# Norm, modulation and router between the output projection and the experts, rebuilt by token, and the last norm joined to the expert rounds

## The reference, cut to what matters

```python
xl = xl + ml[2][:, None] * (merged @ w_out)
h = rms_norm(xl, norm_ffn) * (1 + ml[4]) + ml[3]            # shift and scale differ for context and latent tokens
scores = sigmoid(h @ w_router)                              # 16 experts in 4 groups
# best group by the sum of its top two biased scores, two experts in it, weights normalised
xl = xl + ml[5][:, None] * moe_ffn(h, ...)
y = rms_norm(xl, norm_final)
```

## Time and profile before

| | |
|---|---|
| median of 3 runs | 2398.67 us (2397.53 to 2400.23) |
| the profiled execution | 2402.82 us, of which span 2401.0 us |
| PE, PEld busy | 2188.6 us (91%), 1892.9 us (79%) |
| DVE, ACT, POOL busy | 1483.2, 1143.3, 8.2 us |
| mean granted clock of PE | 0.963 |
| HBM read, written | 453.88 MB, 3.98 MB |

### The profile page before, as it was taken

One profiled execution on the slowest core, in us unless ns is written; L12 is line 12 of the kernel. 1 busy time (PEld: TensorE's weight loads), 2 busy tenths in 40 slices (PEclk: granted clock), 3 DMA queues, 4 the chain that ended last, 5 costly groups with the idle time before them and its releaser, 6 DMA issues. The chain is left out here.

```text
span 2401.0 us, 28904 instructions
## 1 busy us (share of the span) xinstructions
PE 2188.6 (91%) x11236; PEld 1892.9 (79%) x11236; DVE 1483.2 (62%) x2021; ACT 1143.3 (48%) x1534; POOL 8.2 (0%) x12
## 2 busy tenths in 40 slices
PE   7799999999999999998899969965999999999993
PEld 4499988977777899997799968855877777777772
DVE  6967576346544444443544444555678879879984
ACT  6733565333444434332343333332567667667760
POOL 1000000000000000000000000000000000000000
PEclk9899999999999999998999989997899999999996
DMA  9844333433333455543355555520589889889981
GB/s 353 288 148 140 105 139 102 138 123 119 114 115 113 149 179 183 176 167 110 125 182 180 188 177 193 181 90 21 206 287 339 297 287 345 278 309 336 333 294 55
DMA packets 127287, 459.92 MB, mean 192 GB/s; under 512 B 15456, under 2 KB 17280, under 8 KB 126880
## 3 DMA queue, kind: packets, MB, share of 16 engines
q1 hardware_dynamic: 127136, 457.92, 55.3%
HBM read 453.88 MB, written 3.98 MB: 191 GB/s over the span
## 5 line engine op out<-in xcount | busy, mean ns | idle before, releaser
L161 DVE TENSOR_TENSOR wlo<-raw,whi 128x1024 fp32r<-128x1024 f32 x832 | 1006.5, 1223 | 734.7 <-ACT whi L155 720.0
L155 ACT ACTIVATE whi<-raw 128x1024 fp32r<-128x1024 f32 x832 | 870.6, 1058 | 918.6 <-PE bank L173 669.7
L171 PE MATMUL bank<-hhi,whi 128*128 128x384 f32 x1664 | 567.2, 341 | 29.1 <-DVEq L1519 16.9
L173 PE MATMUL bank<-hhi,wlo 128*128 128x384 f32 x1664 | 559.8, 336 | 0.0
L172 PE MATMUL bank<-hlo,whi 128*128 128x384 f32 x1664 | 559.4, 336 | 0.0
L171 PEld LDWEIGHTS bank<-hhi,whi 128*128 128x128 f32 x1664 | 315.2, 189 | 48.5 <-issue 24.9
L172 PEld LDWEIGHTS bank<-hlo,whi 128*128 128x128 f32 x1664 | 315.1, 189 | 1.8
L173 PEld LDWEIGHTS bank<-hhi,wlo 128*128 128x128 f32 x1664 | 314.6, 189 | 0.0
L1994 PE MATMUL bank<-whi,group_hi 128*128 128x512 f32 x512 | 203.6, 398 | 5.3 <-DVE wlo L161 4.0
L1996 PE MATMUL bank<-wlo,group_hi 128*128 128x512 f32 x512 | 201.5, 394 | 0.0
L1995 PE MATMUL bank<-whi,group_lo 128*128 128x512 f32 x512 | 200.5, 392 | 0.0
(11 more groups left out here) (320 smaller groups left out, 2414.6 us busy)
## 6 DMA issues: line engine op xcount, KB each, us to landing
raw<-in_dense SPq DMA_DIRECT2D x448, 512.0 KB, 3.7
raw<-in_moe SPq DMA_DIRECT2D x384, 512.0 KB, 5.0
merged<-in_x SPq DMA_DIRECT2D x8, 768.0 KB, 6.4
cs_rows_bc<-cs_rows SPq DMA_DIRECT2D x8, 768.0 KB, 5.0
out_y<-merged SPq DMA_DIRECT2D x4, 768.0 KB, 3.3
pool_w_sb<-in_pool_w SPq DMA_DIRECT2D x1, 1024.0 KB, 6.2
w_router_sb<-in_w_router SPq DMA_DIRECT2D x1, 1024.0 KB, 4.5
pool_inv_count<-in_pool_inv SPq DMA_DIRECT2D x1, 768.0 KB, 4.3
```

The source lines that it names most:

```text
L155: self.nc.scalar.activation(self.whi[:, n % W, :], self.raw[:, n % R, :], ACT.Copy).then_inc(self.hi_done, 1)
L161: self.nc.vector.tensor_tensor(self.wlo[:, n % W, :], self.raw[:, n % R, :], self.whi[:, n % W, :].bitcast(F32), ALU.subtract).then_inc(se ...
L171: self.nc.tensor.matmul(out, self.whi[:, s, c], xhi[:, k, :], start=(k == 0), stop=False)
L173: last = self.nc.tensor.matmul(out, self.wlo[:, s, c], xhi[:, k, :], start=False, stop=(k == blocks - 1))
```

## The change

1. `w_out_phase`, `norm_phase("ffn")`, `modulate_phase` and `router_phase` become one block, the new `out_phase`. As each block of x is finished within the passes, ACT squares it and writes `u = x * a` (two Copies with a scale for each partition), and DVE adds the squares into one 128x384 sum.
2. After the last tile PE needs three one-column products for the sum over features, now one number for each token in its partition, and rsqrt works on 128x3.
3. 24 units (two feature blocks by 128 tokens): PE multiplies u by `turn` = [identity | w_router], 144 columns, so a unit is token-major u beside its part of the logits; one STT of DVE multiplies by rstd and adds the shift, ACT writes `hhi` and the logit parts, DVE `hlo`. A reduction over 16 parts gives the logits; the chain of choices is as before, without `lows` between its steps.
4. The shift is needed with the features in the columns: it is turned by PE, stored to HBM (16 KB) and loaded back broadcast to all partitions (two DMAs of 1 MB, pieces of 512 B). w_router is loaded as 16 columns of its rows (pieces of 64 B). The shift's share of the logits is computed in pass 1.
5. A round is one block: `pick`, `place` and the slot weights are built in its head. Its tail squares each block of x when it is added (ACT), sums by a float32 product with ones (PE, between the scatters), then makes rsqrt, y and the stores. Rounds 1 and 2 come after that.

```diff
+def out_phase(N, E):
+        @block.sync
+            for s in range(iters * body):
+                N.load(sp, N.tile0 + s + R)
+                if s == 1:
+                    sp.dma_start(E.turn[:, :, P:P + NE], io.w_router[:, :, 0:NE]).then_inc(s_ld, 16)
...
+                if s == 4:
+                    sp.wait_ge(s_rows, 1)
+                    sp.dma_start(flat.rearrange("(q f) -> q f", f=P), E.rows[:, :]).then_inc(s_st, 16)
+                if s == 7:
+                    sp.wait_ge(s_st, 16)
+                    for g in range(2):
+                        sp.dma_start(E.shift[:, g, :, 0:P],
+                                     flat.rearrange("(k g f) -> g k f", g=2, f=P)[g].partition_broadcast(P)).then_inc(s_shift, 16)
...
+        @block.scalar
+            def of_block(m):
+                act.wait_ge(s_x, 4 + 2 * (m + 1))
+                if m >= 2:
+                    act.wait_ge(s_acc, max(1, m - 2))
+                A(E.xsq[:, m % 2, :], xt[:, m, :], ACT.Square).then_inc(s_sq, 1)
+                for g, (lo, hi) in enumerate(SEG):
+                    A(E.u[:, m, lo:hi], xt[:, m, lo:hi], ACT.Copy, scale=N.mod_a[:, m, g:g + 1]).then_inc(s_u, 1)
+            for i in range(iters):
+                for t in range(body):
+                    N.act_hi(act, i, body, t)
...
+                    if i == 0 and t == 3:
+                        A(E.turn[:, :, 0:P], N.ident[:, :].unsqueeze(1).to_broadcast([P, KB, P]), ACT.Copy).then_inc(s_turn, 1)
...
+                    if t - 1 in own_end:
+                        of_block(4 * i + own_end.index(t - 1))
...
+            for n, (q, c) in enumerate(units):
+                act.wait_ge(s_h, n + 1)
+                A(N.hhi[:, 2 * q:2 * q + 2, c * P:(c + 1) * P], E.h[:, n % 4, :, 0:P], ACT.Copy).then_inc(s_hh, 1)
+                A(E.lgp[:, c * NE:(c + 1) * NE, 2 * q:2 * q + 2].rearrange("p e a -> p a e"), E.h[:, n % 4, :, P:P + NE], ACT.Copy)\
+                    .then_inc(s_lg, 1)
...
+        @block.vector
+            for n, (q, c) in enumerate(units):
+                dve.wait_ge(s_mm, n + 1)
...
+                V.scalar_tensor_tensor(out=E.h[:, n % 4, :, :], in0=two(B[ring[q % 2][c]][:, 0:2 * (P + NE)]), scalar=E.ry[:, c:c + 1],
+                                       in1=E.shift[:, seg(c), 2 * q:2 * q + 2, :], op0=ALU.mult, op1=ALU.add).then_inc(s_h, 1)
+                if n >= 2:
+                    low(n - 2)
...
+            V.reduce_sum(E.lt[:, :], E.lgp[:, :, :], AX).then_inc(s_lt, 1)
+            dve.wait_ge(s_ex, 1)
...
+        @block.tensor
+                for b in range(2):
+                    last = mm(bank[:, b * (P + NE):(b + 1) * (P + NE)], E.u[:, 2 * q + b, c * P:(c + 1) * P], E.turn[:, 2 * q + b, :],
+                              start=True, stop=True)
+                last.then_inc(s_mm, 1)
+                if n == 2:
+                    pe.wait_ge(s_acc, KB - 1)
+                    pe.wait_ge(s_x, 2 * KB + 4)
+                    for cc in range(NCH):
+                        last = mm(B[1][:, cc:cc + 1], E.acc[:, cc * P:(cc + 1) * P], N.ones[:, 0:1], start=True, stop=True)
+                    last.then_inc(s_sum, 1)
...
 def expert_round(N, E, r):
+                for lo, hi in ((0, 4), (4, 8), (8, 12), (12, 14), (14, 16)):
+                    sp.wait_ge(E.s_y, KB * r + hi)
+                    sp.dma_start(N.io.y[:, lo:hi, :], E.y[:, lo:hi, :]).then_inc(E.s_out, 16)
...
+                for m in range(KB):
+                    act.wait_ge(E.s_x, (NG - 1 + g0) * KB * 2 + 2 * m + 4)
+                    if m >= 4:
+                        act.wait_ge(E.s_sum, KB * r + m - 3)
+                    A(E.sq[:, m % 4, :], N.merged[:, m, :], ACT.Square).then_inc(E.s_sq, 1)
...
-                for m in range(KB):
-                    scatter(2, 0, m, (6, 7))
+                for m in range(KB + 2):
+                    if m < KB:
+                        scatter(2, 0, m, (6, 7))
+                    if m >= 2:
+                        pe.wait_ge(E.s_sq, KB * r + m - 1)
+                        nc.tensor.matmul(B[0][:, 0:T], N.ones[:, :], E.sq[:, (m - 2) % 4, :], start=(m == 2), stop=(m == KB + 1))\
+                            .then_inc(E.s_sum, 1)
...
-    w_out_phase(N)
-    ffn_phases(N)
-    N.at = N.arena
-    norm_phase(N, "final")
-    out_phase(N)
+    E = Experts(N)
+    out_phase(N, E)
+    for r in range(NCH):
+        expert_round(N, E, r)
```

More of the change, by code:

```diff
@@ L242, in ada_add @@
         .then_inc(s_add, 1)
[L245 to L283, removed]
 def pe_blocks(N, pe, iters):
@@ L1493, in _ @@
             sp.wait_ge(x_in, 64)
[L1496 to L1550, removed]
@@ L1553, in norm_phase @@
[L1553 to L1580, removed]
@@ L1758, in __init__ @@
         self.yhi, self.ylo = sb("ff_out_hi", [P, D], F32R), sb("ff_out_lo", [P, D], F32R)
+        after, N.at = N.at, at
+        self.y = sb("y_normed", [P, KB, T], F32)
+        self.sq = sb("y_squares", [P, 4, T], F32)
+        N.at = at
+        self.shift = sb("shift_rows", [P, 2, KB, P + NE], F32)
+        self.u = sb("x_scaled", [P, KB, T], F32)
+        assert N.at <= kept_top
+        self.h = sb("h_by_token", [P, 4, 2, P + NE], F32)
+        self.rows = sb("shift_turned", [32, P], F32)
@@ L1770, in in_round @@
     return eng.If(eng.value_load(N.most[0:1, 0:1], min_val=0, max_val=T) > P * r)
+STEPS = 13
 def expert_round(N, E, r):
@@ L1875, in group @@
                                 group_high(picked(i, half), p, bank, E.xhi[1 - half])
+                for g in range(NG):
+                    act.wait_ge(E.s_ptr, NG * r + g + 1)
+                    A(E.place[:, g + 1, :], B[g][:, 0:T], ACT.Copy).then_inc(E.s_pl, 1)
                 if r:
+                    act.wait_ge(E.s_out, 80 * r)
                     for t in range(-LEAD, 0):
@@ L1962, in _ @@
                     add_block((NG - 1 + g0) * KB, m, (6, 7)[m % 2])
+                dve.wait_ge(E.s_sum, KB * (r + 1))
+                st.chain(V.tensor_scalar(N.rs_v[:, :], B[0][:, 0:T], 1.0 / D, EPS, ALU.mult, ALU.add))
+                rsqrt_steps(dve, nc, st, N.rs_v[:, :], N.rstd[:, :], N.rs_t[:, :])
+                assert st.n == STEPS * (r + 1)
+                for k in range(KB):
+                    V.scalar_tensor_tensor(out=E.y[:, k, :], in0=N.merged[:, k, :], scalar=N.gains[:, 2, k:k + 1],
+                                           in1=N.rstd[:, :], op0=ALU.mult, op1=ALU.mult).then_inc(E.s_y, 1)
         @block.tensor
```

427 lines of the change are left out of this document (240 added, 187 removed).

## The result

The changed kernel takes 2335.48 us (median of 4 runs, 2331.28 to 2337.35), the kernel before beside it 2398.10 (2396.72 to 2400.23): ratio 0.9730, 95% interval 0.9714 to 0.9746. That is 62.6 us less, where the prediction had 61.0. One execution of a later kernel (the low parts twice) took 7381.68 us and is left out of its times.

What follows compares the result with a forecast made beforehand. PE bounds the output projection; 88.5 us before round 0 and then the end lie on the path. +8 - 51.0 - 0.5 - 17.5 = -61.0 takes the median 2398.67 to 2337.7 us; 8-in-10 range 2329 to 2351.

Steps and rivals of the forecast that it cites:

- The ACT work behind "aaa", +8: Output projection: after three "a" tiles, ACT's new work makes the next "o" tile 1.0 us late, 8 times; bounds 0 to 12.
- DMAs, 0: Output projection: the new loads, store and broadcasts queue with the weight tiles and cost nothing; bound above 4 us.
- the 69 of the rival: Output projection: if load time goes by pieces, w_router's 2048 cost 69 us and hold up weights; 2407 us, chance 0.02.
- Last own tile to the first unit, 5.0: From 1590.3 to 1595.4 us: DVE's additions, ACT's Square, three one-column products, 12 chained steps on three columns.
- The 24 units, 20.8 with the last hand-over: Between projection and chain: DVE sets the pace at 0.85 us per unit, 20.4 in all, plus 0.4 for the last hand-over.
- The chain, 1.3 + 10.3: Before round 0: reduction 0.95 and Exp with hand-over 0.35, then choices 10.3 us, including a wait for counts of 2.8.
- Head, -0.5: Head of round 0: only the barrier between the blocks goes, priced at the 0.54 us of idleness at such a barrier.
- The experts, 0: Expert products: their 630 us are the same instructions on the same tiles.
- Tail, -17.5: From the last scatters to the end: 2383.5 us in place of 2401.0, the norm under the scatters; bounds -20 and -5.
- PE stayed at full clock in the tail: Last scatters: rival that PE stays at 1.2 GHz, 30 us for 17.4, +12.5, giving 2350 us; chance 0.12.
- units did not go at hand-over speed: The 24 units: rival of 1.34 us each, 32.2 us in all, +12, giving 2350 us; chance 0.12.
- the ACT work was not free: Output projection: rival that the new ACT work finds room, 0 for 8, giving 2330 us; chance 0.09.

Runs made afterwards that it cites:

- the low parts twice: Changed kernel with DVE's subtraction for a unit's low part done twice, once into a buffer nothing reads: 2347.10 us (median of three), ratio 0.9768.
- both edits together: Changed kernel with ACT's work per block one tile later and useless products with ones on PE (17 ahead of the counts, two behind, three in round 0's head): 2324.48 us.
- the kernel with 17 and four products: Changed kernel plus products with ones on PE whose result nothing reads, 17 ahead of the counts and four in round 0's head: 2333.97 us, ratio 0.9720.

## Why the prediction was right, point by point

- *The ACT work behind "aaa", +8.* Right in place, number and size: eight waits of 0.94 us, 7.5 in all, and moving the work takes them away. What was missing is that the stage's clock suffers too: the stage grew by 9.9 us in this profiled execution and by 12.4 in the other one of the changed kernel, just over the upper bound of 12. With the order mended the stage is back at 180.0, so all of that hangs on ACT's order.
- *DMAs, 0.* Right. The two broadcasts landed in 9.9 us each and added no wait of PE. Small pieces: 5.4 us for 2048 of them, not the 69 of the rival, and four more such loads left the stage as long as it was. The Trainium skill wants pieces of 512 B or more for line rate (DMA: Bandwidth & Descriptors, Specifications). The trace agrees: 128 KB in pieces of 64 B took 5.4 us to land and a weight tile of 512 KB 3.7 in the median; the ring hid it.
- *Last own tile to the first unit, 5.0.* Measured 5.2 (1595.02 to 1600.20).
- *The 24 units, 20.8 with the last hand-over.* Measured 18.3 (1600.20 to 1618.45). The mechanism is right: DVE without a gap, and doubling one of its two instructions adds 8.1 us, 24 times 0.34. The size is off, since the 0.41 for `low` is the duration of a record, and the records overlap: from start to start it is 0.42 + 0.34, where 0.44 + 0.41 stood. ACT, 13.3 us busy in the same 18.2, and PE, 12.5, don't bind.
- *The chain, 1.3 + 10.3.* Measured 1.3 and 11.1, with a wait for the counts of 2.79 where 2.8 stood. Together -52.6 for -51.0.
- *Head, -0.5.* Measured -1.1. The turned picks (2.82 us) and the slot weights (5.14) are the same in both. PE's wait at the barrier that went was 0.72, not 0.54, which was read from another barrier; most of the rest lies in DVE's first step (0.72 us before, 0.45 now).
- *The experts, 0.* Measured -1.8. From the first pick product to the last expert product the other executions of the changed kernels took 641.3 to 644.0 us; why it was 645.4 before is not shown.
- *Tail, -17.5.* Measured -17.9 in these executions, by a different split. The prediction's own terms hold small slips: 14 scatters of 0.35 and 16 products of 0.66 are 15.5 us, not 15.2; 3.7 us at half clock cost 1.9, not 2.2; and 2373.3 + 0.2 + 9.8 is 2383.3, not 2383.5. They all but cancel. In the trace the loop was 1.8 us shorter, since the half clock expected at its start did not come (in other executions it did), the skips took 11.0 for 9.8, and 0.4 more lies at the barrier ahead of them. The stores (3.1 to 3.3 us each) lay under the skips.
- *The rivals.* PE stayed at full clock in the tail, units did not go at hand-over speed, the ACT work was not free, small pieces were hidden.

So the sum came out 1.6 us from the medians' difference. The mechanisms were right, but so close a sum is partly luck, since its errors have either sign: the projection cost 2 to 4 us more than predicted, and the middle (1.6), the experts (1.8), the head (0.6) and the tail (0.4) gained more. What stays open is at which of the eight waits of the output projection the clock falls: one window shows it in the profiled execution of the changed kernel, several in others.

The best version without useless work is the changed kernel with `of_block` one tile later: 2325.5 and 2330.2 us in two calls, 0.9694 and 0.9693 of before. The 0.9682 with the products added is not told from it.

## What to carry to other kernels

In this kernel, work that was moved beside a stage that PE sets was free only at a point where no engine of the conversion chain is on the path: look for the gapless rows, and put it one tile further. Price a queue of short independent instructions by the distance of their starts, not by the sum of their durations. Mixing a sum into the waits of the scatters was worth 8 us here, as much as everything else that the join of the tail brought.

## What was not expected of the hardware

- PE busy with products of 4 to 16 columns was followed by the clock of 1.2 GHz, as idling was (0.57 in 1622.0 to 1625.5 with PE busy for 3.20 of 3.50 us, both edits together). It isn't always so: in the kernel with 17 and four products, the same counts and slot weights ran, and the clock behind the slot weights stayed at 1.00 (picks of 0.28 us each).
- Waits of 0.94 us in an otherwise busy stage went with stretches at half clock in eight of eight executions, and none came in the four without these waits. At which of the waits it falls is open.
- SP's issue of the DMA behind a load in 64 B pieces took 3.3 us in the changed kernel, and the next two 0.4 each; with four more such loads in a row the issues took 2.3 us each on average.
- The same code got another clock in another execution: the tail's scatters had 0.50 from 2290.0 to 2293.5 in one, and 1.00 throughout in another, 2.6 us apart.
